# Ten one-hot products of an expert pair in one run behind the token transposes, in a 16-pair mixture-of-experts kernel

## What is computed

```python
def run_block(args):
    xb, e = args
    return (jax.nn.silu(xb @ w_eg[e]) * (xb @ w_eu[e])) @ w_ed[e]
...
out = jnp.zeros((T, D_MODEL), jnp.float32).at[t_buf].add(y_buf.astype(jnp.float32) * w_buf[:, None])
```

## Time and profile before

| what | value |
| --- | --- |
| median of 3 runs | 1290.44 us (1290.29 to 1292.85) |
| the profiled execution | 1289.0 us |
| its span, first to last instruction | 1287.1 us |
| tensor engine busy | 1140.2 us (89%) |
| mean granted TensorE clock | 0.943 of full speed |
| start of pair 0 (first transpose) | 756.90 us from the span's start |
| start of the down product of pair 15 | 1229.49 us |

### The profile page before, as it was taken

One profiled execution on the slowest core, in us unless ns is written; L12 is line 12 of the kernel. 1 busy time (PEld: TensorE's weight loads), 2 busy tenths in 40 slices (PEclk: granted clock), 3 DMA queues, 4 the chain that ended last, 5 costly groups with the idle time before them and its releaser, 6 DMA issues.

```text
span 1287.1 us, 16996 instructions
## 1 busy us (share of the span) xinstructions
PE 1140.2 (89%) x6759; PEld 808.4 (63%) x6759; DVE 522.9 (41%) x923; ACT 387.3 (30%) x599; POOL 185.0 (14%) x197
## 2 busy tenths in 40 slices
PE   4899799999999999999999479999999999999942
PEld 3898677787888899999999443333343333333311
DVE  6131577663246555534331622333333433333314
ACT  5312666666556444343321101101011000000102
POOL 7000011110304446422200000000000000000000
PEclk7999899999999999999998769999999999999976
DMA  8364433342212212253360479999999999999902
GB/s 177 58 104 85 79 49 50 50 50 36 64 51 81 67 50 66 75 140 97 98 235 23 185 308 426 429 426 428 427 428 428 428 427 427 429 425 429 382 5 74
DMA packets 96398, 266.89 MB, mean 207 GB/s; under 512 B 4156, under 2 KB 77080, under 8 KB 84040
## 3 DMA queue, kind: packets, MB, share of 16 engines
q1 hardware_dynamic: 89088, 248.00, 54.7%
q0 software_dynamic: 3456, 10.25, 2.1%
q10 hardware_dynamic: 3784, 7.65, 1.7%
HBM read 258.24 MB, written 7.64 MB: 207 GB/s over the span
## 4 chain that ended last, share of the span: by engine, by line
PE 56%; DMA 26%; DVE 8%; ACT 5%; issue 4%; SPq 0%; POOL 0%; ACTq 0%; DVEq 0%; POOLq 0%
DMA arena<-in_w_expert_up 22%; PE za L1068 11%; PE pj L718 10%; PE pj L720 9%; PE pj L719 9%; DMA ring<-in_w_in 3%; PE pj L745 2%; PE zb L1088 2%; DVE arena L1655 1%; DVE arena L1654 1%; PE zb L843 1%; PE ms L1001 1%; ACT arena L1278 1%; PE zb L841 1%; ACT arena L1280 1%
## 5 line engine op out<-in xcount | busy, mean ns | idle before, releaser
L1068 PE MATMUL za<-arena 128*64 128x512 f32 x1024 | 237.7, 620 | 22.8 <-DMA arena<-in_w_expert_up 21.9
L718 PE MATMUL pj<-u_high_r,ring_r 128*128 128x288 f32 x768 | 237.2, 309 | 9.9 <-DVE ring_r L1538 4.8
L719 PE MATMUL pj<-u_rest_r,ring_r 128*128 128x288 f32 x768 | 227.8, 297 | 0.0
L720 PE MATMUL pj<-u_high_r,ring_r 128*128 128x288 f32 x768 | 227.7, 297 | 0.0
L1068 PEld LDWEIGHTS za<-arena 128*64 128x64 f32 x1024 | 74.1, 142 | 178.2 <-issue 143.6
L718 PEld LDWEIGHTS pj<-u_high_r,ring_r 128*128 128x128 f32 x768 | 145.9, 190 | 17.9 <-issue 10.9
L719 PEld LDWEIGHTS pj<-u_rest_r,ring_r 128*128 128x128 f32 x768 | 146.1, 190 | 2.2 <-issue 1.0
L720 PEld LDWEIGHTS pj<-u_high_r,ring_r 128*128 128x128 f32 x768 | 145.7, 190 | 0.0
L1538 DVE TENSOR_TENSOR ring_r<-ring,ring_r 128x1024 fp32r<-128x1024 f32 x68 | 85.6, 1266 | 123.8 <-ACT ring_r L1166 123.7
L1088 PE MATMUL zb<-arena 128*64 128x512 f32 x512 | 113.4, 595 | 4.1 <-DVE arena L1991 3.4
L1088 PEld LDWEIGHTS zb<-arena 128*64 128x64 f32 x512 | 35.9, 137 | 74.6 <-issue 73.3
(11 more groups left out here) (423 smaller groups left out, 2037.7 us busy)
## 6 DMA issues: line engine op xcount, KB each, us to landing
arena<-in_w_expert_gate SPq DMA_DIRECT2D x32, 2048.0 KB, 17.0
arena<-in_w_expert_up SPq DMA_DIRECT2D x32, 2048.0 KB, 17.5
arena<-in_w_expert_down SPq DMA_DIRECT2D x32, 2048.0 KB, 18.4
ring<-in_w_in SPq DMA_DIRECT2D x32, 512.0 KB, 8.5
ring<-in_w_gate SPq DMA_DIRECT2D x24, 512.0 KB, 4.1
arena<-in_x_prompt SPq DMA_DIRECT2D x8, 512.0 KB, 6.6
ring<-in_w_branch_out SPq DMA_DIRECT2D x8, 512.0 KB, 3.3
arena<-in_w_branch_out SPq DMA_DIRECT2D x4, 512.0 KB, 3.4
```

The source lines that it names most:

```text
L718: pe.matmul(out, left[0], right[0], start=k == 0, stop=False)
L719: pe.matmul(out, left[0], right[1], start=False, stop=False)
L720: return pe.matmul(out, left[1], right[0], start=False, stop=k == last - 1)
L1068: m = pe.matmul(za[j * BLK:(j + 1) * BLK, b, :], xT[:, k, j * BLK:(j + 1) * BLK], w[:, j * KD + k, :], start=k == 0, stop=k == KD - 1)
```

## The change

All ten chunks of the preceding pair stand where six stood, on the tensor engine and on VectorE. The two later places are gone. The waits within `scatter` and `add`, and the wait for chunk 7's add before the down product, stay as they are.

```diff
@@ tensor engine, expert_pair @@
                 m.then_inc(S["xt2_ps"], 1)
                 if mix:
-                    scatter(i - 1, range(6), not first)
+                    scatter(i - 1, range(2 * NT), not first)
                 pe.wait_ge(S["xt2_a"], i + 1)
                 pe.wait_ge(S["xt2_d"], i + 1)
...
                     m.then_inc(S[done], 1)
-                if mix:
-                    scatter(i - 1, (6, 7))
                 pe.wait_ge(S["hid_r"], i + 1)
...
                 m.then_inc(S["hidt_ps"], 1)
                 if mix:
-                    scatter(i - 1, (8, 9))
                     pe.wait_ge(S["sc_r"], 2 * NT * (i - 1) + 8)
                 pe.wait_ge(S["hidt_r"], i + 1)
@@ VectorE, expert_pair @@
                 if mix:
-                    add(i - 1, range(6), behind)
+                    add(i - 1, range(2 * NT), behind)
                 dve.wait_ge(S["gate_th"], i + 1)
...
                                          op0=ALU.mult, op1=ALU.mult).then_inc(S["hid_r"], 1)
-                if mix:
-                    add(i - 1, range(6, 10), behind)
                 if over is None:
```

## The result

The changed kernel takes **1297.67 us** in the median of 10 runs (1294.3 to 1299.97), against 1290.9 for the kernel before in the 10 runs beside it: a ratio of **1.0053, 95% interval 1.0038 to 1.0067**, or +6.8 us (4.9 to 8.6). The forecast was +2.2 us and a range up to 1295.2, so the time lies above it. The profiled execution took 1296.6 us with a span of 1294.7, 7.6 us over the span before.

A forecast was written before the change was run, and what follows sets the result against it. Weight arrivals, 30.66 us a pair, were taken to bound the steady part, with only the end uncovered: +2.40 for the front run and -0.21 for the middle gave +2.2 us, 1292.6 us against the median of 1290.44; range 1290.8 to 1295.2.

The forecast's parts named there:

- A: Rival: the clock falls in pair 14's emptied gap, its down product 1.7 us longer; 1294.3, or 1295.1 with lag; chance 0.20.
- B: Rival: the clock falls in every pair, the tensor engine becomes the bound at 31.4 us a cycle; about 1310; chance 0.05.
- the cycle: One down product to the next without waits: 29.75 us against the weights' 30.66, so 0.9 us a pair of cover stays.
- What bounds the kernel: Expert part: weight arrivals, 30.66 us a pair, set the pace; only the start and pair 15 lack that cover.
- The front run: Pairs 1 to 15, ahead of the gate product: four more chunks wait for adds at a 0.60 us pitch, +2.40 us.
- The middle: Between up and down product: removing two times two chunks around the hidden transposes gives back only 0.20 us.
- The start: Pairs 1 and 2: tensor engine 3.0 us late at pair 2's down product, caught up after four pairs, no cost.
- rival C: The DMA queue runs dry at the start and moves all arrivals, up to 2 us on top, 1294.6; chance 0.04.
- The 803.2 of the recorded sum: Start: time in us when pair 1's down load is in, ahead of pair 3's gate load, which must be issued by 800.4.
- if it only falls after waits, it stops itself: Argument on rival B: clock falls that come only after waits end by themselves, as a late engine doesn't wait.
- lag at pair 14: End: pair 14's down product stays fixed at 1201.94 by its down weights, so no lateness there.

The follow-up runs named there:

- the run with the old cover: Against the changed kernel, chunks 6 to 9 of pairs 0 to 14 left out, the other six where they stood before; ratio to the kernel before 1.0011.
- the other profile: A second profile of the changed kernel, nothing changed: eight down products at 8.78 us, 469.68 us from pair 0's down product to the end of pair 15's last `y_rest`.

## Why the prediction was wrong

The sign that the prediction named for A and B, down products at 8.8 us, is there; the step that failed is the cycle, below.

**What bounds the kernel.** Right for the kernel before, and the test of it is the run with the old cover: 12 falls cost nothing there.

**The front run, +2.40 us.** Right. In pair 3 of the changed kernel the gate product starts 6.42 us behind the first transpose of the tokens (849.79 - 843.37), against 4.08 before and 6.5 predicted. The adds keep their pitch of 0.60, as the timeline of VectorE shows:

```profile
845.47 1.28 DVE L1988 TENSOR_TENSOR arena<-arena,pj 128x512 f32<-128x512 f32 x2
846.66 1.28 DVE L1988 TENSOR_TENSOR arena<-arena,zb 128x512 f32<-128x512 f32 x2
847.86 1.27 DVE L1988 TENSOR_TENSOR arena<-arena,pj 64x512 f32<-64x512 f32 x2
849.05 1.27 DVE L1988 TENSOR_TENSOR arena<-arena,zb 128x512 f32<-128x512 f32 x2
850.25 1.27 DVE L1988 TENSOR_TENSOR arena<-arena,pj 128x512 f32<-128x512 f32 x2
```

**The middle, -0.20.** Off by 0.17: up to down product takes 2.45 us in the loop (836.36 - 819.96 - 13.95) against 2.48, so it gives back 0.03. Pair 0's 2.28 had 0.69 us idle ahead of the down product where the loop's pairs have 0.82, an excess that the trace books as issue. What makes it was not tested.

**The start.** Right: pair 2's down product comes 59.63 us behind pair 0's, where its weights came after 823.92 + 10.1 - 777.43 = 56.6 before: 3.0 late, as predicted. The queue did not run dry (rival C): windows from 775 to 840 us show a DMA share of 0.99 to 1.03, and the gate load of pair 3 went out at 797.50. (The 803.2 of the recorded sum should be 784.56 + 15.9 + 2.45 = 802.9; it changes nothing.)

**The cycle: this step failed.** "29.75 us, against 30.66. The cover holds" took the down product at 7.09 in every pair. The free cycle is right, 29.83 measured. But 6 of the 12 cycles from pair 2 to pair 14 had a fall in them: 6 x 29.83 + 6 x 31.52 = 368.1, a mean of 30.67, the weights' own pace to 0.01. So nothing of the 3.0 us was made up. Pair 14's down product, which the prediction held fixed, was 3.2 us late (427.73 us behind pair 0's, against 424.51). That the two paces meet so closely I take for chance, since the other profile, with seven falls in the 14 pairs ahead of pair 15, drifts to 429.53 us behind pair 0 instead of 427.73. That the tensor engine alone sets the cycle shows in the chain, and in the down load of pair 14 as well: issued at 1181.76, with a median landing of 16.3, it was in at about 1200.6 (an estimate: the median, and 2.5 for the second transfer), some 4 us ahead of its use. From 1200 to 1210 us the DMA share is 0.69, where it was 0.97 before: the queue now waits for the tensor engine.

**The rivals.** A had the mechanism and the place, at 0.20, but priced it for pair 14 alone, with a lag of 0.8 us from pair 13. B had the price of a fall in each cycle (31.44 predicted, 31.52 measured) but was all or nothing, 19.5 us at 0.05. The truth lies between: a fall in half the pairs, which the argument "if it only falls after waits, it stops itself" ruled out. It was wrong in that no wait for weights is needed; the waits for VectorE and ScalarE are idle time enough. In the prediction's terms the measured sum is 3.22 (lag at pair 14, put at 0) + 2.29 (pair 14's down product to pair 15's, 29.84 for 27.55 us, put at 2.2) + 1.68 (pair 15's fall, put at 0) = 7.2, all of the 7.2 in S.

**Where the reading went wrong.** Pair 0 was taken as proof that the emptied gaps of every pair do no harm. It was the wrong sample: with 0.85 and 0.69 us idle its down product took 7.09 in all ten profiles, and pair 1 with 0.87 and 0.73 did in the three that emptied both of its gaps. The loop's pairs have 0.87 and 0.82, and of those 14 pairs 7 and 8 fell in the two profiles of the changed kernel. Whether the 0.1 us more is what matters, and what picks the pairs that fall, no run shows. The section of the Trainium skill that was weighed against pair 0, "Why this matters for your kernels" in "TensorE: Matmul & The Clock Gate", named the right danger: this trace agrees that idle gaps between matmuls bring half rate, at 8.78 us for 7.09. But the gap that it warns of is longer than either piece here or than both together, so it doesn't give these falls; the measurement goes beyond it. The danger was given a fifth of the chance because pair 0 spoke against it.

## What to carry to other kernels

Work that stands in the tensor engine's waits is not worth its own duration there but what it holds up: here 1.8 us of one-hot products cost 0.03 us in the gaps of the loop and 2.3 us in a run where they queue for four banks, and they kept the clock from falling behind the gaps besides. Before moving such filler away, count the idle pieces that it leaves in a short stretch together, and price a fall of the clock per pass of the loop, against the cover per pass, not once. Where the cover is as thin as such falls make it, a late start stays late to the end: pace against pace decides, not the size of the delay.

## What I had not expected of the hardware

Two idle pieces of 0.87 and 0.82 us with four transposes (0.75 us) between them brought the clock down in 22 of 42 pairs of the loop (three profiles with all ten chunks in front and no filler, pairs 2 to 15), while 1.27 us in one piece brought it down in none of 12 when the other piece was filled, and 0.87 with 1.6 us did in 12 of 13. A single matmul in each piece was enough for none in 14.
